# Prompt-stage barriers, loads and state moves, and narrower query products, in a one-core decoder step

## The chip, the cores and the metric

One core of one Trainium2 chip runs the whole program in one launch. The metric is device microseconds of one execution, median of the runs shown. The core's engines are TensorE (PE in the rows, PEld for its weight loads), VectorE (DVE), ScalarE (ACT), GpSimd (POOL) and SyncE (SP). Each runs its own list of instructions in order; they meet through semaphores. SP and GpSimd issue the DMAs, which all share 16 DMA engines.

## The reference

One layer of a decoder for a prompt of 512 positions and for 8 sequences with 4 new positions each (32 rows), model width 1024:

```
p   = x @ w_in                                   # q, k, v of 8 stick-breaking and 8 dilated-window heads
o   = concat(stick_breaking(...), merged dilated windows(...))
h1  = LayerNorm1(alpha * x + o @ w_out)
q   = (h1 @ peer_wq).reshape(tokens, 8, 2, 128)  # the query products
s   = einsum('nhcd,ckd->nhck', q, subkeys)       # 128 scores; top 16 of each, then top 16 of the 16 x 16 sums
y   = LayerNorm2(alpha * h1 + sum over the chosen experts e of gelu(h1 . u[e]) * gate * v[e])
```

Besides y it returns the new keys and values, and for each of the 8 sequences the window state (2048 rows of keys and as many of values), of which all but four rows are the old state shifted by four: that shift is a copy from memory to memory.

## The kernel before

All is float32. Where a product is split into a high and a low part (type FP32R), three products stand for one: high x high, high x low, low x high. The 544 tokens (512 and 32) lie in five tiles of 128, of which the last has 32 rows and 96 of padding.

The program is a list of stages. In each, every engine has a part, and `end_stage` closes it: the engine drains, adds 1 to the semaphore `over`, and waits until all five engines have done so. The stages that matter here, with the stretch of the profiled execution:

- **Projections** (0 to 209.8 us). SP loads x in one DMA, then the sample rows, the 128 x 640 constants `square` (identity, triangle, ones), the angles, and 24 blocks of `w_in`. TensorE transposes x into four PSUM banks, ScalarE copies the high part, VectorE subtracts the low part, and a bank is free for TensorE again when VectorE is done with it. VectorE begins with clearing buffers. GpSimd stores keys and values as they come out, the dilated keys and values with nine DMAs each.
- **Stick-breaking heads of the prompt** (209.8 to 310.9). SP loads the bias and `counts` (1 MB). For each of 8 heads TensorE makes the scores, VectorE the logits (L666), ScalarE the logarithms and exponents, TensorE the suffix sums, and at last TensorE weighs the values (L604) and ScalarE copies the result (L644).
- **Dilated heads of the prompt** (310.9 to 377.0): scores (L710), logits on VectorE (L770), exponents, transposes, weighing; then the results are transposed into `o_t` (ScalarE L815). Their buffers lie where those of the stage before lay.
- **Samples** (377.0 to 872.8): the 8 sequences against their pages and windows.
- **Norm** (872.8 to 965.1): SP loads the two rows of LayerNorm1, the subkeys and the first two blocks of `peer_wq`. TensorE multiplies each of five tiles by `w_out` (L1419), VectorE adds and normalises, TensorE transposes the result (L1410), which is split into parts: three tiles into `h1_r` and the other two, 256 columns, into `h1_rest`. TensorE is up to two tiles ahead of VectorE.
- **Query** (from 965.1): 8 blocks of `peer_wq` of 1 MB, two buffers. For each of 16 chunks of 128 query columns TensorE makes 24 products of 384 token columns and 24 of the rest (L1563), then the scores of the chunk before (L1548, plain f32). ScalarE copies; VectorE finds the top 16 of each score row. Block g + 2 is loaded when the low part of block g has been made. ScalarE's order has the high part of block 2 ahead of its copy of the first scores, and VectorE's has the first top-16 ahead of the low part of block 2. No barrier stands behind this stage: gates and experts follow as data allow.

The shift of the window state is 16 copies of 4 MB (`move_state`, L565), which GpSimd issues in four portions, `MOVES`, in the stages of the stick-breaking heads (once the counts are in), of the dilated heads, of the norm and of the query. After each portion GpSimd comes to its `end_stage`, but for the last.

Of the kernel before, what the change touches and what calls it, by code (L numbers as in the profile page):

```python
# [38 lines left out]
DB, DT = 8, 4  # L39
NS = DB * DT  # L40
N = SEQ + NS
NT = 5
NP = NT * P
H, HD = 8, 64
# [12 lines left out]
ND = 3 * P  # L57
# [108 lines left out]
def build(nc, x_prompt, x_sample, cache_k_sb, cache_v_sb, page_table, state_k_win, state_v_win,  # L166
# [4 lines left out]
    with ExitStack() as ctx:  # L171
# [75 lines left out]


        over = sem("stage_over")
        stage = {}  # L250

        def end_stage(eng):

            name = eng.engine
            stage[name] = stage.get(name, 0) + 1
            eng.drain().then_inc(over, 1)
            eng.wait_ge(over, 5 * stage[name])

        def clear_semaphores(sp):

# [37 lines left out]
        xs_rows = x_sample.rearrange("b t d -> (b t) d")  # L298
        w_in_g = w_in.rearrange("(e k p) (g c) -> g e p k c", e=2, p=P, c=WC)
        NG_IN = 2 * len(GROUPS)  # L300

        def rows_of(t):
            return P if t < NT - 1 else NS
# [6 lines left out]

        @part("sp")
        def _(sp):
            sp.dma_start(x_nat[:, 0:4, :], x_rows).then_inc(sem("x_prompt_in"), 16)
            sp.wait_ge(sem("tail_cleared"), 1)
            sp.dma_start(x_nat[0:NS, 4, :], xs_rows).then_inc(sem("small_in"), 16)
            sp.dma_start(sq, square).then_inc(sem("square_in"), 16)
            sp.dma_start(cos_sb, cosine).then_inc(sem("angles_in"), 16)
            sp.dma_start(sin_sb, sine).then_inc(sem("angles_in"), 16)
            sp.dma_start(pages_sb[:, :], page_table.rearrange("b j -> (b j)").rearrange("(o n) -> o n", o=1))\
              .then_inc(sem("pages_in"), 16)  # L320
            for g in range(NG_IN):
                for e in range(2):
                    if g >= 1:
                        sp.wait_ge(sem("w_low"), 2 * (g - 1) + e + 1)
                    sp.dma_start(w_sb[e], w_in_g[2 * COLUMN[GROUPS[g // 2]] + g % 2, e]).then_inc(sem(f"w_in_{e}"), 16)
# [27 lines left out]
        @part("pe")  # L353
        def _(pe):
            pe.wait_ge(sem("square_in"), 16)
            for t in range(NT):
                pe.wait_ge(sem("x_prompt_in" if t < 4 else "small_in"), 16)
                r = rows_of(t)
                for half in range(2):
                    u = 2 * t + half  # L360
                    if u >= 4:
                        pe.wait_ge(sem("x_low"), u - 3)
                    for k in range(4):
                        last = pe.transpose(bank(u % 4)[:, k * P:k * P + r],
                                            x_nat[0:r, t, (4 * half + k) * P:(4 * half + k + 1) * P],
                                            ident[0:r, 0:r])
                    last.then_inc(sem("x_t_ready"), 1)
            pe.wait_ge(sem("x_low"), 10)

            def turn(c, tiles):  # L370

                if c < 2:
                    pe.wait_ge(sem("proj_copied"), 10 * c + 10)
                else:
                    pe.wait_ge(sem("roped"), c - 1)
                for t in tiles:
                    v = 5 * c + t
                    if v >= 4:
                        pe.wait_ge(sem("qk_copied_dve"), v - 3)
                        if (v - 4) // 5 % 2 == 0:  # L380
                            pe.wait_ge(sem("q_copied_act"), 5 * ((v - 4) // 10) + (v - 4) % 5 + 1)
                    r = rows_of(t)
                    for pair in range(NPAIR):
                        last = pe.transpose(bank(4 + v % 4)[:, pair * P:pair * P + r],
                                            staged[c % 2][0:r, t, pair * P:(pair + 1) * P], ident[0:r, 0:r])
                    last.then_inc(sem("qk_ready"), 1)

            for c in range(len(GROUPS)):
                for g in (2 * c, 2 * c + 1):
                    pe.wait_ge(sem("w_low"), 2 * g + 2)  # L390
                    for t in range(NT):
                        u = NT * g + t
                        if u >= 4:
                            pe.wait_ge(sem("proj_copied"), u - 3)
                        r = rows_of(t)
                        n = 0
                        for k in range(KD):
                            for x, y in PARTS:
                                n += 1
                                last = pe.matmul(bank(u % 4)[0:r, 0:WC], lhsT=x_r[:, x, k, t * P:t * P + r],  # L400
                                                 rhs=w_in_r[g % 2][:, y, k, :], start=(n == 1), stop=(n == 3 * KD))
                        last.then_inc(sem("proj_ready"), 1)

                        if t == 1 and g % 2 == 0 and 2 <= c <= 5:
                            turn(c - 2, (NT - 1,))
                if 1 <= c <= 4:
                    turn(c - 1, range(NT - 1))
# [148 lines left out]
        bias = small[:, 0:8]  # L556
        bias_ht = small[:, 8:40].rearrange("p (h t) -> p h t", h=H)

        MOVES = (7, 4, 3, 2)

        def move_state(pool, turn):
            for n in range(sum(MOVES[:turn]), sum(MOVES[:turn + 1])):
# [123 lines left out]
                if h + 1 < H:  # L686
                    softplus(h + 1)

        for engine in programs:
            programs[engine].append(end_stage)  # L690


        PT_AT = (0, 1, 3, 6)
        dl_p = [take(WIDE, WORK)] + [take(WIDE)]
        dl_t = [take(WIDE) for _ in range(2)]
# [8 lines left out]
        @part("pe")  # L704
        def _(pe):
            def scores(h):
                if h >= 1:
                    pe.wait_ge(sem("dl_logits"), 4 * h)
                for qb in range(KB):
                    last = pe.matmul(bank(qb)[:, 0:(qb + 1) * P], lhsT=q_z["dil"][:, h, qb * P:(qb + 1) * P],  # L710
                                     rhs=k_t["dil"][:, h // 2, 0:(qb + 1) * P], start=True, stop=True)
                last.then_inc(sem("dl_scores"), 1)

            def weigh(h):
                pe.wait_ge(sem("dl_turned"), h + 1)
                if h >= 1:
                    pe.wait_ge(sem("dl_out_scaled"), h)
                for qb in range(KB):
                    for kb in range(qb + 1):
                        a = (PT_AT[qb] + kb) * P  # L720
                        c = qb * HD
                        last = pe.matmul(bank(7)[:, c:c + HD], lhsT=dl_t[h % 2][:, a:a + P],
                                         rhs=v_n["dil"][:, kb, h * HD:(h + 1) * HD], start=(kb == 0), stop=(kb == qb))
                last.then_inc(sem("dl_out"), 1)

            scores(0)
            for h in range(H):
                if h + 1 < H:
                    scores(h + 1)
                pe.wait_ge(sem("dl_exp"), 4 * h + 4)  # L730
                if h >= 1:
                    pe.wait_ge(sem("dl_turned"), h)
                for j in range(10):
                    last = pe.transpose(bank(4, 3)[:, j * P:(j + 1) * P], dl_p[h % 2][:, j * P:(j + 1) * P], ident)
                last.then_inc(sem("dl_turn"), 1)
                if h >= 1:
                    weigh(h - 1)
            weigh(H - 1)
# [21 lines left out]
        def _(dve):  # L760
            dve.wait_ge(sem("counts_in"), 2 * 16)

            def logits(h):

                dve.wait_ge(sem("dl_scores"), h + 1)
                if h >= 2:
                    dve.wait_ge(sem("dl_turn"), h - 1)
                for qb in range(KB):
                    a, w = PT_AT[qb] * P, (qb + 1) * P
                    dve.tensor_tensor_reduce(out=dl_p[h % 2][:, a:a + w], in0=bank(qb)[:, 0:w], in1=counts[:, qb, 0:w],  # L770
                                             scale=SCALE, scalar=LOWEST, op0=ALU.add, op1=ALU.max,
                                             accum_out=dl_max[h % 2][:, qb:qb + 1]).then_inc(sem("dl_logits"), 1)
                dve.wait_ge(sem("dl_logits"), 4 * h + 4)
                dve.tensor_scalar(dl_neg[h % 2], dl_max[h % 2], -1.0, None, ALU.mult).then_inc(sem("dl_neg"), 1)
# [34 lines left out]

        @part("act")  # L810
        def _(act):
            for u in range(8):
                t, half = u // 2, u % 2
                act.wait_ge(sem("o_t_ready"), u + 1)
# [653 lines left out]

        COLS = (ND, H1_REST)
        NC = 2 * PH
        NWQ = NC // 2
        place[0] = KEPT
# [58 lines left out]
        def _(pe):  # L1533
# [18 lines left out]
            for c in range(NC):  # L1552
                pe.wait_ge(sem("w_low"), 2 * NG_IN + c // 2 + 1)
                w = wq_r[c // 2 % 2]
                for half in range(2):
# [4 lines left out]
                    for x, y in PARTS[::-1]:  # L1560
                        for k in range(KD):
                            n += 1
                            last = pe.matmul(bank(u % 4)[:, 0:COLS[half]], lhsT=w[:, x, k, c % 2 * P:(c % 2 + 1) * P],  # L1563
                                             rhs=(h1_r, h1_rest)[half][:, y, k, :],
                                             start=(n == 1), stop=(n == 3 * KD))
                    last.then_inc(sem("pq_ready"), 1)
                if c >= 1:
# [787 lines left out]
```

## Time and profile before

| | us |
|---|---|
| median of 3 runs | 2494.16 (2484.43 to 2496.2) |
| profiled execution, its own time | 2485.89 |
| its span, first to last instruction | 2484.1 |
| TensorE busy | 2298.1 |
| VectorE busy | 1548.5 |
| ScalarE busy | 940.5 |
| GpSimd busy | 390.8 |

The profile is that of one execution. Busy time is an engine's own; waiting for a semaphore is not busy. A timeline row gives the start, the duration, the engine, the line, the operation, what is written from what, the number of instructions merged, and in brackets the idle time before it with what ended it. The landing of a DMA is counted from its issue.

### The profile page before, as it was taken

What the parts mean: (1) busy time and instruction counts of PE and PEld (TensorE: products, weight loads), DVE (VectorE), ACT (ScalarE), POOL (GpSimd) and SP (SyncE); (2) the same over time, 40 slices, a digit from 0 to 9 for tenths busy, and PEclk for the clock granted to TensorE, in tenths of its full rate; (3) what the DMA queues carried; (4) which work ended last, traced back from release to release, by engine and by line L of the source; (5) the groups of instructions that cost most, each with busy time, mean ns of one, the idle gap of its engine ahead of it and who ended that gap; (6) DMA issues with size and microseconds to landing.
All of it is one profiled execution on the core that took longest, in us unless ns stands there. A gap on an engine that the chain in (4) does not pass through costs nothing.

```text
span 2484.1 us, 37894 instructions
## 1 busy us (share of the span) xinstructions
PE 2298.1 (93%) x12921; PEld 1896.2 (76%) x12921; DVE 1548.5 (62%) x3167; ACT 940.5 (38%) x1432; POOL 390.8 (16%) x370
## 2 busy tenths in 40 slices
PE   7997887999999788998999879999999999999996
PEld 7996674666666436985577779999999999999995
DVE  3342331344434423769898877777777777777777
ACT  3224643445444401223356623333333333333332
POOL 0001000000000000000000043333333333333330
PEclk9998888989989888999999989999999999999998
DMA  4226985766666574303355699999999999999982
GB/s 129 87 88 204 304 270 186 233 194 208 209 212 215 171 255 143 97 25 97 99 197 183 235 344 322 314 314 313 313 315 313 311 312 311 314 313 312 311 294 82
DMA packets 224063, 568.20 MB, mean 229 GB/s; under 512 B 18017, under 2 KB 96418, under 8 KB 221282
## 3 DMA queue, kind: packets, MB, share of 16 engines
q1 hardware_dynamic: 174946, 327.75, 39.9%
q0 software_dynamic: 49024, 239.23, 27.7%
q8 instruction: 56, 0.92, 0.2%
q14 instruction: 37, 0.30, 0.0%
HBM read 528.24 MB, written 105.12 MB: 255 GB/s over the span
## 4 chain that ended last, share of the span: by engine, by line
PE 71%; DVE 6%; DMA 4%; SPq 2%; ACT 2%; issue 2%; DVEq 0%; ACTq 0%
PE psum L2067 21%; PE psum L2055 16%; PE psum L1842 6%; PE psum L1563 3%; PE psum L2045 3%; PE psum L999 3%; PE psum L1865 3%; PE psum L1071 2%; PE psum L1053 2%; PE psum L989 2%; PE psum L1419 2%; PE psum L1021 2%; DMA sample<-in_cache_v_sb_dram 1%; DMA peer<-in_ln_b_dram 1%; DMA peer<-in_peer_wq_dram 1%
## 5 line engine op out<-in xcount | busy, mean ns | idle before, releaser
L2067 PE MATMUL psum<-expert_parts 128*128 128x512 f32 x2304 | 550.5, 395 | 0.0
L2067 PEld LDWEIGHTS psum<-expert_parts 128*128 128x128 f32 x2304 | 427.0, 189 | 86.3 <-issue 0.8
L2055 PE MATMUL psum<-h_parts,expert_parts 128*128 128x384 f32 x2304 | 444.2, 341 | 2.9 <-DVE expert_parts L2172 1.5
L2055 PEld LDWEIGHTS psum<-h_parts,expert_parts 128*128 128x128 f32 x2304 | 402.9, 189 | 10.9 <-issue 1.8
L2119 ACT ACTIVATE expert_parts<-peer 128x1024 fp32r<-128x1024 f32 x128 | 135.8, 1061 | 359.1 <-PE psum L2067 322.2
L2172 DVE TENSOR_TENSOR expert_parts<-psum,expert_parts 128x512 fp32r<-128x512 f32 x192 | 132.7, 691 | 151.4 <-ACT expert_parts L2113 151.4
L2215 DVE SCALAR_TENSOR_TENSOR kept<-experts,kept 128x1024 f32<-128x1024 f32 x160 | 205.0, 1281 | 5.3 <-DVE kept L2205 3.0
L2030 POOL DMA_INDIRECT experts<-in_peer_v_dram,kept x160 | 188.5, 1178 | 70.1 <-issue 47.5
L1842 PE MATMUL psum<-h_whole,gate_table 128*128 128x384 f32 x512 | 179.0, 493 | 13.8 <-ACT gate_table L1894 13.8
L1326 DVE TENSOR_TENSOR sample_parts<-sample,sample_parts 128x512 fp32r<-128x512 f32 x128 | 85.1, 690 | 157.5 <-ACT sample_parts L1179 157.0
L400 PE MATMUL psum<-projection_parts 128*128 128x256 f32 (+1 forms) x1440 | 173.5, 282 | 3.8 <-DVE projection_parts L506 3.8
L400 PEld LDWEIGHTS psum<-projection_parts 128*128 128x128 f32 (+1 forms) x1440 | 169.6, 174 | 5.9 <-issue 3.9
L2113 ACT ACTIVATE expert_parts<-psum 128x512 fp32r<-128x512 f32 x192 | 115.0, 599 | 149.5 <-PE psum L2045 142.9
L2177 DVE TENSOR_TENSOR expert_parts<-peer,expert_parts 128x1024 fp32r<-128x1024 f32 x128 | 155.9, 1218 | 0.0
L1842 PEld LDWEIGHTS psum<-h_whole,gate_table 128*128 128x128 f32 x512 | 93.0, 192 | 69.9 <-issue 19.7
L2025 POOL DMA_INDIRECT experts<-in_peer_u_dram,kept x96 | 95.2, 992 | 322.8 <-DVE experts L2199 188.9
L1155 ACT ACTIVATE sample<-psum 128x512 f32<-128x512 f32 x128 | 75.9, 593 | 161.5 <-PE psum L989 161.3
L2025 POOL DMA_INDIRECT peer<-in_peer_u_dram,kept x62 | 80.4, 1297 | 357.7 <-DVE peer L2199 352.1
L999 PEld LDWEIGHTS psum<-attention,sample 128*128 128x128 f32 x1024 | 133.1, 202 | 1.4 <-issue 0.8
L2045 PE MATMUL psum<-kept,peer 128*128 128x128 f32 x768 | 116.1, 274 | 16.6 <-DVE expert_parts L2172 16.1
L999 PE MATMUL psum<-attention,sample 128*128 (+1 forms) x1024 | 129.4, 253 | 0.0
L2199 DVE SCALAR_TENSOR_TENSOR experts<-experts,kept 128x1024 f32<-128x1024 f32 x96 | 116.8, 1219 | 0.0
(281 smaller groups left out, 3261.9 us busy)
## 6 DMA issues: line engine op xcount, KB each, us to landing
peer<-in_peer_v_dram SPq DMA_DIRECT2D x128, 512.0 KB, 5.2
peer<-in_peer_u_dram SPq DMA_DIRECT2D x96, 512.0 KB, 5.4
sample<-in_cache_k_sb_dram SPq DMA_DIRECT2D x128, 256.0 KB, 3.1
sample<-in_cache_v_sb_dram SPq DMA_DIRECT2D x128, 256.0 KB, 2.9
out_dram<-in_state_k_win_dram POOLq DMA_DIRECT2D x8, 4088.0 KB, 35.6
out_dram<-in_state_v_win_dram POOLq DMA_DIRECT2D x8, 4088.0 KB, 33.8
gates_dram<-gate_table SPq DMA_DIRECT2D x12, 2048.0 KB, 7.1
experts<-gates_dram SPq DMA_DIRECT2D x32, 768.0 KB, 6.9
```

The lines of the kernel that those rows point to most:

```text
L400: last = pe.matmul(bank(u % 4)[0:r, 0:WC], lhsT=x_r[:, x, k, t * P:t * P + r], rhs=w_in_r[g % 2][:, y, k, :], start=(n == 1), stop=(n == 3 ...
L999: last = pe.matmul(bank(2)[:, c:c + 8].rearrange("p (e t) -> p e t", e=2), lhsT=k_turned[j % 2][:, pair, :], rhs=q_s["sb"][:, 2 * pair:2 * ...
L1842: last = pe.matmul(bank(6)[:, 0:ND], lhsT=early_t[e % 2][:, k, :], rhs=h1_f[:, k, :], start=(k == 0), stop=(k == KD - 1))
L2025: pool.indirect_dma_start(out=u_rows[p], out_offset=None, in_=peer_u, in_offset=index(q, p))\
L2030: pool.indirect_dma_start(out=v_rows[p], out_offset=None, in_=peer_v, in_offset=index(q - 1, p))\
L2045: last = pe.transpose(bank(7)[:, k % 4 * P:(k % 4 + 1) * P], u_sb[s][:, k * P:(k + 1) * P], ident)
L2055: last = pe.matmul(bank(6)[:, 0:ND], lhsT=u_t[s][:, a, k, :], rhs=h1_r[:, b, k, 0:ND], start=(k == 0 and n == 0), stop=(k == KD - 1 and n ...
L2067: last = pe.matmul(bank(2 * t + half), lhsT=weight[s][:, a, t * P:(t + 1) * P], rhs=v_r[s][:, b, half * 512:(half + 1) * 512], start=(firs ...
L2119: act.activation(v_r[s][:, 0, :], v_sb[s], ACT.Copy).then_inc(sem("v_high"), 1)
L2172: dve.tensor_tensor(u_t[s][:, 1, ks, :], bank(7).rearrange("p (k j) -> p k j", k=4), u_t[s][:, 0, ks, :], ALU.subtract).then_inc(sem("u_lo ...
L2177: dve.tensor_tensor(v_r[s][:, 1, :], v_sb[s], v_r[s][:, 0, :], ALU.subtract).then_inc(sem("v_low"), 1)
L2215: dve.scalar_tensor_tensor(y, v_rows[p], dots_act[:, p:p + 1], y, ALU.mult, ALU.add).then_inc(sem("added"), 1)
```

## The change

- GpSimd takes no part in the first barrier (`WITHOUT_POOL`); ScalarE waits for the stores of the dilated keys before it writes `o_t`, which lies over their buffer.
- The second barrier, between stick-breaking and dilated heads, is gone. In its place the dilated stage waits for single semaphores: TensorE's first scores, its first transposes, and VectorE's first two heads of logits.
- `square` is loaded first, and the x of the prompt in four DMAs, one per tile, each with its semaphore.
- `MOVES` goes from 7, 4, 3, 2 to 11, 0, 0, 5.
- The second products of each query chunk take 160 token columns (32 + 128) in place of 256; the 96 columns of padding are left out, in the products and in ScalarE's copy. `h1_rest` keeps its size.

```diff
+        WITHOUT_POOL = (1,)
         stage = {}
         def end_stage(eng):
             name = eng.engine
             stage[name] = stage.get(name, 0) + 1
+            if eng is nc.gpsimd and stage[name] in WITHOUT_POOL:
+                return
             eng.drain().then_inc(over, 1)
-            eng.wait_ge(over, 5 * stage[name])
+            eng.wait_ge(over, 5 * stage[name] - len([n for n in WITHOUT_POOL if n <= stage[name]]))
...
+        X_IN = ("x_prompt_in", "x_in_1", "x_in_2", "x_in_3", "small_in")
...
-            sp.dma_start(x_nat[:, 0:4, :], x_rows).then_inc(sem("x_prompt_in"), 16)
+            sp.dma_start(sq, square).then_inc(sem("square_in"), 16)
+            for t in range(4):
+                sp.dma_start(x_nat[:, t, :], x_rows[:, t, :]).then_inc(sem(X_IN[t]), 16)
             sp.wait_ge(sem("tail_cleared"), 1)
             sp.dma_start(x_nat[0:NS, 4, :], xs_rows).then_inc(sem("small_in"), 16)
-            sp.dma_start(sq, square).then_inc(sem("square_in"), 16)
...
-                pe.wait_ge(sem("x_prompt_in" if t < 4 else "small_in"), 16)
+                pe.wait_ge(sem(X_IN[t]), 16)
...
-        MOVES = (7, 4, 3, 2)
+        MOVES = (11, 0, 0, 5)
...
-        for engine in programs:
-            programs[engine].append(end_stage)
...
             def scores(h):
                 if h >= 1:
                     pe.wait_ge(sem("dl_logits"), 4 * h)
+                else:
+                    pe.wait_ge(sem("sb_logits"), H)
+                    pe.wait_ge(sem("sb_exponents"), H)
...
                 if h >= 1:
                     pe.wait_ge(sem("dl_turned"), h)
+                else:
+                    pe.wait_ge(sem("sb_out_copied"), H)
                 for j in range(10):
...
                 if h >= 2:
                     dve.wait_ge(sem("dl_turn"), h - 1)
+                else:
+                    dve.wait_ge(sem("sb_out"), H - 1 + h)
                 for qb in range(KB):
...
         def _(act):
+            act.wait_ge(sem("k_dil_out"), (1 + DB) * 16)
             for u in range(8):
...
-        COLS = (ND, H1_REST)
+        COLS = (ND, N - ND)
...
-                                             rhs=(h1_r, h1_rest)[half][:, y, k, :],
+                                             rhs=(h1_r, h1_rest)[half][:, y, k, 0:COLS[half]],
```

## Rows read from the trace of the kernel before

**Rows 1.** The page, busy time, share of the span and instructions of the engines.
```profile
PE 2298.1 (93%) x12921; PEld 1896.2 (76%) x12921; DVE 1548.5 (62%) x3167; ACT 940.5 (38%) x1432; POOL 390.8 (16%) x370
```
**Rows 2.** Table of stretches: stretch, length, busy us, granted clock, DMA share, GB/s.
```profile
872.80:965.10 92.30, 78.85 (x200) 37.24 (x200) 33.03 (x46) 11.11 (x22) 1.48 (x3) 0.89 0.52 172
965.10:1112.00 146.90, 139.83 (x933) 133.81 (x934) 86.54 (x465) 37.13 (x57) 0.99 (x2) 0.96 0.33 108
```
**Rows 3.** Timeline, start of the projections, VectorE.
```profile
13.00 5.20 DVE L512 TENSOR_TENSOR projection_parts<-psum,projection_parts 128x512 fp32r<-128x512 f32 x10
...
18.38 2.36 DVE L506 TENSOR_TENSOR projection_parts<-prompt,projection_parts 128x1024 fp32r<-128x1024 f32 x2 [0.18 <-ACT projection_parts L427]
```
**Rows 4.** GpSimd's drains, stretches 190:215 and 215:315 (ns min/median/max, first and last start).
```profile
L256 POOLq DRAIN  x1: 4057/4057/4057, 205.8 to 205.8; - x1
...
L256 POOLq DRAIN  x2: 52547/72128/91708, 219.1 to 312.7; - x2
```
**Rows 5.** Timeline around the first three barriers.
```profile
201.58 0.37 ACT L453 ACTIVATE attention<-psum 32x256 f32<-32x256 f32 x1 [2.36 <-PE psum L400]
...
209.87 0.35 SPq L573 DMA_DIRECT2D kept<-in_sb_logit_bias_dram  x1
...
215.92 1.55 DVE L666 TENSOR_SCALAR prompt_attention<-psum,kept 128x1280 f32<-128x1280 f32 x1 [34.11 <-DMA prompt_attention<-in_count_prompt_dram]
216.42 0.54 POOL L565 DMA_DIRECT2D out_dram<-in_state_k_win_dram  x1 [9.41 <-DMA prompt_attention<-in_count_prompt_dram]
...
303.24 0.38 ACT L644 ACTIVATE prompt_attention<-psum 128x256 f32<-128x256 f32 x1 [3.58 <-PE psum L604]
310.90 3.92 PE L710 MATMUL psum<-prompt 128*128 128x128 f32 x8 [7.70 <-SPq L256]
...
315.00 0.29 DVE L770 CUSTOM_DVE_ANT_0 prompt_attention<-psum,prompt_attention 128x128 f32<-128x128 f32 x1 [16.92 <-PE psum L710]
...
372.25 2.56 ACT L815 ACTIVATE kept<-psum 128x512 f32<-128x512 f32 x5 [0.17 <-PE psum L806]
```
**Rows 6.** DMA view, issues at 216.4, 873.2 and 969.4 us: KB, us to landing.
```profile
out_dram<-in_state_k_win_dram POOLq DMA_DIRECT2D x1, 4088.0 KB, 15.8
...
peer<-in_ln_b_dram SPq DMA_DIRECT2D x1, 512.0 KB, 30.3
...
peer<-in_peer_wq_dram SPq DMA_DIRECT2D x1, 1024.0 KB, 27.7
```
**Rows 7.** Timeline, norm stage, TensorE.
```profile
872.85 29.43 PE L1419 MATMUL psum<-w_out_sb,kept 128*128 128x512 f32 x64 [1.89 <-DVEq L256]
...
909.55 1.97 PE L1410 MATMUL psum<-kept 128*128 128x128 f32 x8 [7.28 <-DVE kept L1384]
...
911.32 15.59 PE L1419 MATMUL psum<-w_out_sb,kept 128*128 128x512 f32 x32
...
926.74 1.04 PE L1410 MATMUL psum<-kept 128*128 128x128 f32 x8
...
927.62 13.90 PE L1419 MATMUL psum<-w_out_sb,kept 128*128 128x512 f32 x32
```
**Rows 8.** DMA view, stretch 974:990: queue, packets, MB, share of 16 engines.
```profile
q0 software_dynamic: 96, 5.23, 99.6%
q1 hardware_dynamic: 96, 0.10, 3.1%
```
**Rows 9.** Timeline, query stage (and one weighing, 296.39).
```profile
296.39 2.34 PE L604 MATMUL psum<-attention,prompt_attention 128*128 128x64 f32 x20
...
969.43 81.86 SPq L1530 DMA_DIRECT2D peer<-in_peer_wq_dram  x6
...
994.05 1.16 PE L1548 MATMUL psum<-peer,kept 128*128 128x128 f32 x8
...
999.21 3.03 PE L1563 MATMUL psum<-h_rest,wq_parts 128*128 128x256 f32 x24
...
1006.76 6.00 PE L1563 MATMUL psum<-h_parts,wq_parts 128*128 128x384 f32 x24 [3.10 <-DVE wq_parts L1611]
```

## The prediction

> **What bounds the kernel now.** I read the page first. TensorE is busy 93% of the span and no other engine comes near it [rows 1], so on the whole TensorE sets the time; but the edits sit in the first 1.1 ms, where the table of stretches shows gaps [rows 2]: in the norm stage (872.8 to 965.1 us) TensorE is busy for 78.9 of 92.3 us, in the query stage (to 1112.0) for 139.8 of 146.9. Then I followed the order of time through each stage that the diff touches, and last the landings of the DMAs. Each stretch ends in another wait, so each edit has its own price.
>
> **Start: square first, x in four pieces.** TensorE's first transposes wait for the square now, so an earlier start looks worth some us. But VectorE clears buffers up to 13.0 us, then subtracts the x parts without a gap to 18.2, and the first weight part follows with 0.18 us of idle [rows 3]. TensorE's fifth group of transposes waits for VectorE's first subtraction (four banks), so whatever comes sooner in front of VectorE only waits there. I take 0; the cover is VectorE's clearing, and at most 0.2 us can come out. SP issues three more DMAs ahead of the first weight load, some 1.4 us, and that load is wanted at 17.3 us; 0 again.
>
> **First barrier without GpSimd.** GpSimd's drain before it runs from 205.8 to 209.9, since it holds until its stores of the last values have landed [rows 4]. ScalarE's last copy, which follows TensorE's last product, ends at 202.0. SP issues its next load at 209.87, the counts follow 0.4 later, and VectorE's first logits start at 215.92, when the counts land [rows 5]. Without GpSimd the barrier opens at about 202.5 (that copy and a short drain), the counts are issued at 202.9 and, at the same 5.6 us, land at 208.5. They now share the DMA engines with 1 MB of the values' stores: the bounds are 208.5 (no collision) and 210.7 (what is left of those stores goes first, 2.2 us). I take 209.6: **6.3 us gained**, between 5.2 and 7.4. ScalarE's new wait on the stores of the dilated keys, before the last transposes' copies, is for stores issued in mid-projections; 0.
>
> **Second barrier removed.** ScalarE's last copy of the stick-breaking heads starts at 303.24 and takes 0.4, yet TensorE starts the dilated scores only at 310.90 [rows 5]. The reason is again GpSimd's drain: it starts at 219.1 and takes 91.7 us, to 310.8, the landing of the seventh move of window state [rows 4]. After the change TensorE goes from the last weighing, which ends as that copy begins, straight to the scores, behind waits on values that this weighing has needed itself. They take 3.9 us as here, less if the clock stays up, so VectorE's first dilated logits start at 305.7 to 307.1 and not at 315.00. **8.5 us gained**, 7.9 to 9.3. The new waits of VectorE (previous head's weighing) and of TensorE's transposes (last copy, 303.6) end before that.
>
> **The moves of window state: 7, 4, 3, 2 become 11, 0, 0, 5.** GpSimd issues a move in 0.5 us; the first lands 15.8 us after its issue at 216.42, at 232.2, the seventh at 310.8, so one move takes (310.8 - 232.2) / 6 = 13.1 us [rows 4 to 6]. Eleven, issued from 210.1, end at 210.1 + 15.8 + 10 x 13.1 = 356.9. GpSimd's drain holds the next barrier until then; the other engines reach it when the copies that end at 374.81 are done [rows 5], now 14.8 us sooner, at 360.0. Cost 0, with 3 us of cover; should the moves be slower, each us beyond that is lost.
>
> In the norm stage three moves stand on the DMA engines when SP loads the norm's rows. The second of these rows lands after 30.3 us [rows 6], VectorE waits for it, and TensorE, two tiles ahead, stands for 7.28 us and then runs one turn at 1.97 us and one tile at 15.59, where the later ones take 1.04 and 13.90 [rows 7]. With no move there the row, half the size of the counts, lands in their 5.6 us or less, tile 0 is normalised some 6 us after its products are done (888 + 6 = 894), and TensorE, busy with tile 1 until 902.3, does not wait: 7.3 + 0.9 + 1.7 = **9.9 us gained** (7.3 if the two slow pieces stay).
>
> In the query stage five moves stand where two stood. Here the third weight block is issued at 969.43 and lands after 27.7 us, at 997.1 [rows 6, 9]. Why it is held can be counted: from 974 to 990 us the moves' queue passed 96 packets with 5.23 MB, the completion words among them, and SP's queue 96 with 0.10 MB [rows 8]. The queues alternate packet by packet, the moves' packets are some 64 KB and the load's 1 KB, and the load has 1024 of them. ScalarE waits for this block ahead of the first scores' copy, so VectorE's first top-16 and its low part of that block come later too, and TensorE's fifth chunk starts at 1006.76, 9.6 us after the landing, with 3.10 us of idle [rows 9]. Three moves more put all of this back by 3 x 13.1 = **39.3 us lost**. TensorE has its four chunks done at 1002 now and nothing else in its order. Nothing takes it back later: from here VectorE's top-16 follows TensorE chunk by chunk, and the gates follow VectorE. A page of the Trainium skill would have it otherwise: "DMA: Bandwidth & Descriptors", section "Queues, rings and completion order", says that an engine drains a packet of some 9 to 17 descriptors of one queue before it switches; by that the block's 64 pieces per engine would need 4 to 7 turns and land before five moves are through, with a sum of 2518. The row of 96 against 96 speaks for one piece a turn.
>
> **160 columns.** 16 chunks x 24 products go from 256 to 160 columns. At 256 the 24 take 3.03 us with the tail, 2.96 to the next instruction. What 160 cost no row shows: every FP32R product of this trace has 256 columns or more. From below: products of 64 columns, each a load of 128 weights and a product, run 20 in 2.34 us, 117 ns each [rows 9], so the loads hold the pace: 24 x 117 = 2.81 us, 0.15 less per chunk. If the loads didn't, 160/256 of 2.96 is 1.85, 1.1 less. From above: a plain f32 product of 512 columns costs two instructions, 32 in 13.90 us [rows 7], that is 869 ns or 1.70 ns per column; at this rate 160 columns are 272 ns, 24 of them 6.5 us, **3.55 us more per chunk**. The nearest rows in width, 128 columns, are all plain f32 and priced like that (8 instructions, four products, 1.16 us with the tail) [rows 9]; the pace of one column per cycle I see at 256 and up alone. I take the upper price and keep both ends. The first four chunks pay it inside the wait for the third weights (4 x 3.55 = 14 of 44 us idle); the other twelve pay 12 x 3.55 = **42.6 us lost**. ScalarE's shorter copies are behind TensorE; 0.
>
> A page speaks against this choice: the Trainium skill's "FP8 and Floating Point Precision", section "TensorE Precision Notes", gives four passes to true FP32 only and has reduced FP32 read as it is and truncated, without a word on width; by it the sum would be 2499. No row here has such a product.
>
> **Sum**, against the profiled execution, 2485.9 us with a span of 2484.1: -6.3 - 8.5 - 9.9 + 39.3 + 42.6 = +57.2, so 2543. The median of the three runs is 2494.2 (2484.4 to 2496.2), 8 above that execution; I name the sum's own figure.
>
> **The rivals.**
> - **The narrow products are not dear.** They run at the pace of the weight loads: -24.7 + 39.3 - 12 x 0.15 = +12.8, 2499; with nothing holding them -24.7 + 39.3 - 13.2 = +1.4, 2487. For it: at 256 columns a product takes 123 ns, hardly more than the 117 of one with 64 columns, so width itself may cost little. Against it: no FP32R width below 256 is shown. This one mechanism ends on the other side, within 0.5% of before; the point is a product of 117 ns, where 123 is the price now.
> - **The five moves do not hold the third weights.** The block then lands in time, and all 16 chunks pay the columns: -24.7 + 16 x 3.55 = +32, 2518. Against it: two stages show loads held, 30.3 us under three moves, 27.7 under two. It decides if the landing stays under some 30 us after the issue.
> - **Both of these:** -24.7 - 16 x 0.15 = -27, 2459, the one way to a faster kernel.
> - **The eleven moves hold the barrier** (slower by their lateness beyond 3 us): a few us on top of the forecast, inside its range.
>
> **Chances and range.** The forecast 0.58, with its own range 2530 to 2556 (ends of the gains together 4 us either way, a column price some 15% off, the median's 8 us). Cheap columns 0.27, weights not held 0.07, both 0.05, the rest 0.03. About 0.5%, 12.5 us, is what a measurement of this kernel can tell from no change. Cheap columns fall around that bound: I split them, 0.15 within and 0.12 slower. So faster 0.05, same 0.16, slower 0.79. From 2488 to 2556 lie the forecast, cheap columns and unheld weights, less some tails.
>
> **What would show each step.** VectorE's first logits near 209.6; dilated logits about 3 us after the copy at 303.24 starts there (11.8 now); GpSimd's drain to about 357; no wait on the norm's row; the third weights landing about 71 us after the query stage's start (32 now) and the fifth chunk at about 81; 24 narrow products in 6.5 us (or 2.8). The forecast is wrong if that last figure is near 2.8, or if the fifth chunk starts near 42 us into the stage.

## The result, and the profile after

| | kernel before | changed kernel |
|---|---|---|
| median | 2494.07 us (8 runs, 2484.43 to 2496.53) | 2509.38 us (8 runs, 2504.91 to 2512.23) |
| profiled execution | 2485.9 us, span 2484.1 | 2506.44 us, span 2504.6 |
| ratio | | 1.0069, 95% interval 1.0052 to 1.0086 |

Slower, as forecast, and inside the whole range (2488 to 2556), but below the forecast's own (2530 to 2556): by 15 us and not by 57. The median lies nearest to the rival "the narrow products are not dear" (+12.8 us). The changed lines stand some 5 to 9 lines further down than before (the query products are L1572, were L1563).

First the table of the two stretches that [rows 2] show for before: the norm stage and the query stage (their columns are those of [rows 2]).

```profile
866.10:948.20 82.10, 75.86 (x200) 35.93 (x200) 33.12 (x46) 11.24 (x23) 0.00 (x0) 0.96 0.12 40
948.20:1130.90 182.70, 138.22 (x929) 132.75 (x930) 85.71 (x459) 35.22 (x55) 2.46 (x5) 0.85 0.47 156
```

The norm stage lost its gap. In the query stage TensorE is busy for about as long as before, yet the stage has grown by some 36 us: the new time is idle time, not dearer products.

The start, and the first three stages, in the timeline (against [rows 3] and [rows 5]):

```profile
5.28 1.94 PE L369 MATMUL psum<-kept 128*128 128x128 f32 x8 [5.28 <-DMA kept<-in_x_prompt_dram]
...
13.00 3.21 DVE L517 TENSOR_TENSOR projection_parts<-psum,projection_parts 128x512 fp32r<-128x512 f32 x5
...
13.77 4.64 PE L369 MATMUL psum<-kept 128*128 128x128 f32 x24 [4.51 <-DVE projection_parts L517]
...
22.20 2.05 PE L405 MATMUL psum<-projection_parts 128*128 128x256 f32 x8 [3.80 <-DVE projection_parts L511]
...
203.28 0.37 ACT L458 ACTIVATE attention<-psum 32x256 f32<-32x256 f32 x1 [2.36 <-PE psum L405]
...
210.94 1.55 DVE L671 TENSOR_SCALAR prompt_attention<-psum,kept 128x1280 f32<-128x1280 f32 x1 [27.43 <-DMA prompt_attention<-in_count_prompt_dram]
...
298.02 4.58 PE L714 MATMUL psum<-prompt 128*128 128x128 f32 x8
298.26 0.38 ACT L649 ACTIVATE prompt_attention<-psum 128x256 f32<-128x256 f32 x1 [3.40 <-PE psum L609]
...
302.74 0.29 DVE L778 CUSTOM_DVE_ANT_0 prompt_attention<-psum,prompt_attention 128x128 f32<-128x128 f32 x1 [9.46 <-PE psum L714]
...
360.71 2.56 ACT L824 ACTIVATE kept<-psum 128x512 f32<-128x512 f32 x5 [0.26 <-PE psum L814]
...
365.54 0.18 DVE L1195 COPY kept<-kept 128x32 f32<-128x32 f32 x1 [8.59 <-SPq L266]
```

TensorE's rows of before, at the start:

```profile
10.14 6.95 PE L364 MATMUL psum<-kept 128*128 128x128 f32 x40 [10.14 <-DMA kept<-in_square_dram]
20.89 3.34 PE L400 MATMUL psum<-projection_parts 128*128 128x256 f32 x15 [3.80 <-DVE projection_parts L506]
```

TensorE turns x 5 us sooner, but VectorE still takes its first part at 13.00. TensorE stands 4.51 us for it, and its first projection product starts 1.3 us later than before. From ScalarE's last copy to the first logits are now 7.66 us (14.34 before), from the last stick-breaking copy to the first dilated logits 4.48 (11.76 before): both barriers are open sooner.

GpSimd's drain behind the eleven moves (ns min/median/max, first and last start):

```profile
L259 POOLq DRAIN  x1: 144676/144676/144676, 215.9 to 215.9; - x1
```

It ends at 215.9 + 144.7 = 360.6, before ScalarE's last copy at 363.27: the moves hold nothing here. TensorE's timeline of the norm stage, against [rows 7]:

```profile
866.17 29.20 PE L1428 MATMUL psum<-w_out_sb,kept 128*128 128x512 f32 x64 [1.90 <-DVEq L259]
...
895.21 1.04 PE L1419 MATMUL psum<-kept 128*128 128x128 f32 x8
896.08 13.90 PE L1428 MATMUL psum<-w_out_sb,kept 128*128 128x512 f32 x32
```

The wait of 7.28 us is gone, and the two slow pieces have become 1.04 and 13.90. The timeline of the query stage, which ScalarE begins at 948.20, against [rows 9]:

```profile
982.61 2.80 PE L1572 MATMUL psum<-h_rest,wq_parts 128*128 128x160 f32 x24
...
1019.26 1.91 ACT L1586 ACTIVATE wq_parts<-peer 128x2048 fp32r<-128x2048 f32 x1 [49.97 <-DMA peer<-in_peer_wq_dram]
...
1028.84 6.33 PE L1572 MATMUL psum<-h_parts,wq_parts 128*128 128x384 f32 x24 [3.92 <-DVE wq_parts L1620]
```

Two things can be read here. The fourth chunk's products are done at 985, and the fifth starts at 1028.84, 80.6 us into the stage (41.7 before), behind ScalarE's 50 us of waiting for the third weight block. And 24 products of 160 columns take 2.80 us, not the 6.5 of the forecast. The DMA view: the third block's landing, and the two queues between 972.5 and 992.5 (packets, MB, share of the engines), against [rows 6] and [rows 8]:

```profile
peer<-in_peer_wq_dram SPq DMA_DIRECT2D x1, 1024.0 KB, 66.7
...
q0 software_dynamic: 128, 6.28, 94.3%
q1 hardware_dynamic: 128, 0.13, 2.7%
```

The 2.80 us are the sign that the prediction named for being wrong. So the theory to test: the five moves cost the query stage some 39 us, the removed waits give back some 24, and the columns cost nothing. Its rivals: something other than the moves holds the third block; the columns are dear after all and hide in the stall.

### The profile page after: what moved, and what is told of

It is laid out like the page before. It is cut to its first block, busy times and chain, and to the rows that moved or that the text cites. A ratio compares the mean times of both kernels' runs of the same rounds, so it can differ in the third digit from the quotient of the medians.

```text
span 2504.6 us, 37893 instructions
## 1 busy us (share of the span) xinstructions
PE 2300.9 (92%) x12921; PEld 1899.6 (76%) x12921; DVE 1548.9 (62%) x3167; ACT 939.0 (37%) x1432; POOL 390.3 (16%) x370
## 4 chain that ended last, share of the span: by engine, by line
PE 81%; DVE 7%; ACT 3%; SPq 3%; DMA 2%; issue 2%; another core or an unknown queue 2%; DVEq 0%; ACTq 0%
PE psum L2076 20%; PE psum L2064 16%; PE psum L405 7%; PE psum L1851 6%; PE psum L1572 4%; PE psum L2054 3%; PE psum L1008 3%; PE psum L1874 3%; PE psum L1428 3%; PE psum L1080 2%; PE psum L1062 2%; PE psum L998 2%; DMA sample<-in_cache_v_sb_dram 2%; PE psum L1030 1%
```

## The experiments

**The five moves, put elsewhere.**

```diff
-        MOVES = (11, 0, 0, 5)
+        MOVES = (11, 0, 5, 0)
...
+            pool.wait_ge(sem("norms_in"), 2 * 16)
             move_state(pool, 2)
```

> The changed kernel with the five moves issued in the norm stage behind the landing of the norm's two rows, and none in the query stage. Theory (the moves alone hold the third weight block, the columns cost nothing): the third block lands some 12 us or less after its issue (66.7 in the changed kernel), TensorE does not stand before its fifth chunk, the query stage goes from 179.7 us back to 136 to 140, and the time is some 43 us under the changed kernel's 2509: 2466, 0.989 of before. Rival 1 (the stall is only moved): the first two weight blocks, or GpSimd's drain, are not through when the norm stage would end, and the stage grows by 10 us or more: 2480. Rival 2 (the narrow products cost the plain rate after all, hidden in the stall): 16 x 3.55 = 57 us come back out of it, 2520.

Measured: 2464.27 us, 0.9891 of before (0.986 to 0.9922). The query stage, from ScalarE's first weight copy to the last product's start, takes 135.7 us, where the changed kernel takes 179.9 and before 143.2; the norm stage stays at 82.1. TensorE's timeline at the fifth chunk, the landing of the third block, and GpSimd's drain behind the moves:

```profile
984.90 2.80 PE L1573 MATMUL psum<-h_rest,wq_parts 128*128 128x160 f32 x24
987.63 0.41 PE L1555 MATMUL psum<-peer,kept 128*32 128x128 f32 x2
987.97 1.16 PE L1558 MATMUL psum<-peer,kept 128*128 128x128 f32 x8
988.88 4.41 PE L1573 MATMUL psum<-h_parts,wq_parts 128*128 128x384 f32 x24
...
peer<-in_peer_wq_dram SPq DMA_DIRECT2D x1, 1024.0 KB, 5.5
...
L259 POOLq DRAIN  x1: 68012/68012/68012, 876.5 to 876.5; - x1
```

The block lands in 5.5 us and TensorE goes from chunk to chunk. The drain ends at 944.5, 6 us before ScalarE begins the query stage (950.48), so the moves are hidden where they now stand. They hold another load instead, the second weight block, issued at 870.24:

```profile
peer<-in_peer_wq_dram SPq DMA_DIRECT2D x1, 1024.0 KB, 74.5
```

It lands at 944.75 and is wanted only in the query stage, so this costs nothing, with less than 6 us to spare. The rivals fall: nothing else held the third block, the stall is not moved into the norm stage, and no dear columns came to light when it went.

**Fewer moves in front of the block.**

```diff
-        MOVES = (11, 0, 0, 5)
+        MOVES = (11, 0, 2, 3)
```

> The changed kernel with two of the five moves in the norm stage (not held back) and three in the query stage. Theory (each move ahead of the third block costs 13.1 us): the block lands 66.7 - 2 x 13.1 = 40.5 us after its issue and the fifth chunk starts at 80.4 - 26.2 = 54 us of the stage; the norm stage loses up to 10 us to the held row again, so 2509 - 26 + 7 = 2490, 0.998 of before. Rival (the block waits for all moves of a batch, or something else than the moves holds it): fifth chunk still near 80 us, time 2505 or more.

Measured: 2489.73 us, 0.9995 (0.9977 to 1.0014). The DMA view's landings of the third block and of the norm's second row:

```profile
peer<-in_peer_wq_dram SPq DMA_DIRECT2D x1, 1024.0 KB, 40.6
...
peer<-in_ln_b_dram SPq DMA_DIRECT2D x1, 512.0 KB, 30.1
```

The fifth chunk starts 54.5 us into the stage. With 27.7 us under two moves [rows 6], 40.6 under three and 66.7 under five, each move more costs 13 us, as the forecast had it. The norm's row is the other way: two moves hold it for 30.1 us, three for 30.3 [rows 6], and the norm stage takes 91.4 us again. The row goes in packets of 4 KB (127 with 0.50 MB in a stretch of the first experiment where no move runs), 128 for its 512 KB. Two moves are as many: 4088 KB in packets of 64 KB are 64 a move. It is also as many as one piece in the next experiment, which lands after 29.3 us. So the row lands with the second move, however many follow, and two moves cost the norm stage as much as three.

**The third block in eight pieces.**

```diff
+                pieces = [slice(k, k + 1) for k in range(KD)] if g == 2 else [slice(0, KD)]
+                for ks in pieces:
+                    sp.dma_start(wq_sb[g % 2][:, ks], wq_g[g][:, ks]).then_inc(sem(f"w_in_{g % 2}"), 16)
```

ScalarE's wait on the block counts the eight pieces.

> The changed kernel with the third weight block loaded in eight pieces of 128 packets of 1 KB instead of one load of 1024, so that each piece's landing is seen. Theory (the two queues pass packet for packet, some 5.5 a us each while moves run: 208 of the load's packets in 38 us in the changed kernel): the first piece lands some 23 us after its issue, the second some 46, and the other six together just after the last move, near 67; nothing changes in the time, 2505 to 2509. Rival 1 (a load stands wholly behind the moves that were issued before it): the first piece too lands only near 60 us or later. Rival 2 (each turn passes some ten of the load's packets): all eight are in by 30 us, and the stall goes.

Measured: 2499.71 us, a single run beside a single one of before, 2492.25, and so below the 2505 to 2509 expected; the fifth chunk still starts 80.5 us into the stage. Landings of the first and second piece and the median of two later ones; then the queues of 966 to 986 us, while the moves run, and of 1006 to 1014, when they end:

```profile
peer<-in_peer_wq_dram SPq DMA_DIRECT2D x1, 128.0 KB, 29.3
...
peer<-in_peer_wq_dram SPq DMA_DIRECT2D x1, 128.0 KB, 51.6
...
peer<-in_peer_wq_dram SPq DMA_DIRECT2D x2, 128.0 KB, 61.0
...
q0 software_dynamic: 135, 6.74, 98.5%
q1 hardware_dynamic: 137, 0.12, 3.0%
...
q1 hardware_dynamic: 1733, 1.67, 63.2%
q0 software_dynamic: 21, 0.33, 11.0%
```

The second piece takes 22.3 us longer than the first; the other six land between 1008.9 and 1013.5, around the end of the last move at 1010.6. Neither rival fits. The first two pieces are some 6 us later than I expected; why is open. Equal counts of packets (135 and 137) would also come of ten for ten, but the trace's single packets show turns of one: in the changed kernel, from 955 to 1010 us, where a packet starts just as another ends, the two are of different queues in 585 of the 595 cases that can be told. The section "Queues, rings and completion order" of the Trainium skill's page "DMA: Bandwidth & Descriptors", with its 9 to 17 descriptors (a typical figure, it says) drained from one queue before a switch, is not borne out by these two queues.

**The columns, back to 256 and alone.**

```diff
-        COLS = (ND, N - ND)
+        COLS = (ND, H1_REST)
```

> The changed kernel with 256 columns again in the query products of the last tiles. Theory (the pace of the weight loads, 117 ns a product at 160 columns against 123 at 256): 24 products take 3.03 us, not 2.80; four of the 16 chunks lie inside the stall, so 12 x 0.23 = 2.8 us more than the changed kernel: 2512, 1.008 of before. Rival (the price of my forecast, 272 ns a product): 43 us less, 2467.

> The kernel before with the 160 columns alone. Theory (pace of the weight loads): 24 products in 2.80 us instead of 3.03, of which the first four chunks' part goes into the wait for the third block: 12 x 0.23 = 2.8 us less, 0.999 of before, not to be told from it by the time. Rival (my forecast's price): 24 products in 6.5 us, the time 43 to 57 us up, 1.017 to 1.023 of before.

Measured: 2506.86 us, 1.0063 (1.0045 to 1.0081) for 256 columns in the changed kernel, and 2489.77, 1.0001 (0.9983 to 1.0018) for 160 in the kernel before. The groups of 24 products in TensorE's timelines, first of the one and then of the other:

```profile
1050.29 3.03 PE L1572 MATMUL psum<-h_rest,wq_parts 128*128 128x256 f32 x24
```

```profile
1021.53 2.80 PE L1563 MATMUL psum<-h_rest,wq_parts 128*128 128x160 f32 x24
```

The query stage takes 183.1 us with the 256 columns against 179.9 in the changed kernel, and 140.4 with 160 alone against 143.2 before: 3 us either way, near the 12 x 0.23 of the theory. So small a difference does not show in the medians. The 43 us of the forecast's price would have shown in both.

**The same 160 columns as plain f32.**

```diff
-  lhsT=w[:, x, k, c % 2 * P:(c % 2 + 1) * P],
-  rhs=(h1_r, h1_rest)[half][:, y, k, 0:COLS[half]],
+  lhsT=w[:, x, k, c % 2 * P:(c % 2 + 1) * P].bitcast((F32R, F32)[half]),
+  rhs=(h1_r, h1_rest)[half][:, y, k, 0:COLS[half]].bitcast((F32R, F32)[half]),
```

> The changed kernel with the 160-column products of the last tiles read as plain f32, so the type alone differs (their result is more exact, nothing is left out). Theory (the price of my forecast was the price of the other type): two instructions a product at 1.70 ns a column, 272 ns, so 24 products take 6.5 us instead of 2.80 and the 12 chunks outside the stall cost 12 x 3.7 = 44 us: 2550, some 1.024 of before. Rival (at 160 columns plain f32 goes by the pace of weight loads too, two instructions of 117 ns): 24 in 5.6 us, 12 x 2.8 = 34 us: 2540.

Measured: 2551.61 us, 1.024 (1.0223 to 1.0257). TensorE's timeline, 24 products and what follows:

```profile
1047.64 6.68 PE L1572 MATMUL psum<-h_rest,wq_parts 128*128 128x160 f32 x48
1054.26 0.41 PE L1554 MATMUL psum<-peer,kept 128*32 128x128 f32 x2
```

Twice the instructions, and (1054.26 - 1047.64) / 24 = 276 ns a product; the forecast had 272. So the price was right for plain f32, and the forecast put it on the wrong type.

**Narrower still.**

```diff
-        COLS = (ND, N - ND)
+        COLS = (ND, 64)
```

> The changed kernel with 64 columns in the query products of the last tiles: the queries of the last 96 tokens are left out, the copies of them too. Theory (the load of 128 weights sets the pace from 160 columns down): 24 products still take 2.80 us, 117 ns each. Rival (the columns still count): down by the same 0.23 us per 96 columns, 2.57 us.

Measured: 2506.88 us, a single run. This kernel leaves out the queries of the last 96 tokens. The group in TensorE's timeline:

```profile
1038.69 2.76 PE L1572 MATMUL psum<-h_rest,wq_parts 128*128 128x64 f32 x24
1041.38 0.41 PE L1554 MATMUL psum<-peer,kept 128*32 128x128 f32 x2
```

To the next instruction 2.69 us at 64 columns, 2.73 at 160, 2.96 at 256: 112, 114 and 123 ns a product. From 160 columns down the width hardly counts, and the rival's 2.57 us is not met; this fits a load of 128 weights that sets the pace, which no run changes by itself. The floor lies a little under the 117 ns of [rows 9].

**The two barriers, each alone in the kernel before.** One has the changed `end_stage` with `WITHOUT_POOL = (1,)` and ScalarE's wait on `k_dil_out`; the other leaves out the second `end_stage` and has the four waits that replace it.

> The kernel before with the first barrier without GpSimd (and ScalarE's wait on the stores of the dilated keys). Theory: from the end of ScalarE's last copy of the projections to VectorE's first logits 14.0 us become 7.3, as in the changed kernel, and GpSimd's drain still opens the second barrier, at the landing of the seventh move, which is issued 5 to 7 us sooner: so the time goes 5 to 7 us down, 0.9975 of before. Rival (the seventh move's landing does not come sooner, and the second barrier takes the gain back): dilated logits at 315 as before, no change.

> The kernel before without the second barrier. Theory: from the last stick-breaking copy to VectorE's first dilated logits 11.8 us become 4.5, as in the changed kernel, and GpSimd's drain, now behind eleven moves from 216.4, ends at 216.4 + 15.8 + 131 = 363 while the others are done at 367: 7.3 us gained at both the dilated logits and the sample stage's start, 0.997 of before. Rival (the eleven moves hold the next barrier): the sample stage starts at 377 as before, and nothing is gained.

Measured: 2483.43 us, 0.9968 (0.9953 to 0.9982), and 2484.0 us, 0.998 (0.9958 to 1.0002). Timeline of the first, at the second barrier:

```profile
304.27 4.23 PE L713 MATMUL psum<-prompt 128*128 128x128 f32 x8 [7.36 <-SPq L259]
```

Timeline of the second there, and GpSimd's drain in it:

```profile
304.75 0.38 ACT L644 ACTIVATE prompt_attention<-psum 128x256 f32<-128x256 f32 x1 [3.23 <-PE psum L604]
...
309.23 0.29 DVE L773 CUSTOM_DVE_ANT_0 prompt_attention<-psum,prompt_attention 128x128 f32<-128x128 f32 x1 [9.29 <-PE psum L709]
...
L256 POOLq DRAIN  x1: 141098/141098/141098, 222.0 to 222.0; - x1
```

With the first edit alone TensorE still stands 7.36 us for the drain, but the drain opens 6.6 us sooner than before (304.27 against 310.90), so this barrier does not take the gain back. From its first logits to the sample stage's first copy the dilated stage takes 61.9 to 66.7 us over all profiles, 62.1 before and 65.7 in this one, so only 2.7 us are left of it at the sample stage's start in this execution; the median is 6 us down. With the second alone the copy-to-logits time is the 4.48 us of the changed kernel, and the drain ends at 363.1, as worked out beforehand, ahead of the other engines (370.2). The interval of its ratio reaches 1, so its gain is shown by the profile rather than by the time.

**What covers the start.**

```diff
-            (four clearings of q_z, ahead of the x subtractions)
             w_low(0)
+            (the same four clearings)
             w_low(1)
...
-            act.wait_ge(sem("staged_cleared"), 7)
+            act.wait_ge(sem("staged_cleared"), 3)      # and 7 in q_copy
```

> The changed kernel with VectorE's four long clearings of the query buffers moved behind its first weight part (ScalarE's wait on them moved to its first copy into those buffers). Theory (VectorE's clearing is what the earlier x waits for): the first subtraction starts at 7 to 8 us instead of 13.0, ScalarE's and VectorE's turn of 0.86 us a half then ends near 16, and TensorE's first projection product starts at 18 to 19 instead of 22.2: 3 to 4 us gained in the profile, hardly to be told by the time (1.005 of before). Rival (the weights' load, or ScalarE, holds the first product): still 21 us or later.

> The same clearings moved, but x in one load and the square behind it, as in the kernel before: the first transposes still start near 10.1 us. Theory (with the cover gone, the order of the loads is worth what TensorE starts sooner): the first projection product 2 to 4 us later than in the run with the new order. Rival (something behind the transposes holds both): the same start in both.

Measured: 2499.41 us, 1.0043 (1.0021 to 1.0065), and for the old loads a single run, 2496.89 beside a median of 2488.9 before. The intervals overlap with the changed kernel's, so the profiles decide. Timeline with the new order of loads, and then with the old one:

```profile
7.07 0.69 DVE L514 TENSOR_TENSOR projection_parts<-psum,projection_parts 128x512 fp32r<-128x512 f32 x1 [3.52 <-ACT projection_parts L421]
...
16.34 7.94 PE L405 MATMUL psum<-projection_parts 128*128 128x256 f32 x43 [4.48 <-DVE projection_parts L508]
```

```profile
20.82 3.49 PE L403 MATMUL psum<-projection_parts 128*128 128x256 f32 x16 [3.80 <-DVE projection_parts L506]
```

The first projection product starts at 16.34, 5.9 us sooner than in the changed kernel and sooner than the 18 to 19 expected. With the old loads and the same clearings it starts at 20.82, where before it was 20.89. Neither edit gives anything without the other.

**Both edits that helped.** The moves of the first experiment and the clearings of this one:

> The five moves in the norm stage behind the norm's rows, and the clearings moved: both edits at once. Theory (the two lie in stages that do not touch): 2464 - 3.5 = 2460, 0.9875 of before. Rival (the sooner start is lost again at the barrier that GpSimd's eleven moves hold, whose cover is 3 us): 2464, 0.989.

Measured: 2450.7 us, 0.9841 (0.9818 to 0.9865), the fastest of all. That is some 9 us better than expected. The start gives 5.2 us of it instead of 3.5 (first projection product at 16.97); the rest I cannot assign beyond the spread of its runs (2448.36 to 2456.79).

## Why the forecast was right in its sign and wrong in its size

| step of the prediction | forecast, us | profile, us | |
|---|---|---|---|
| start | 0 | +1.3 | covered by the clearings, but not free |
| first barrier without GpSimd | -6.3 | -6.7 | right |
| second barrier removed | -8.5 (-7.9 to -9.3) | -7.3 | right cause, a little less in this profile |
| eleven moves | 0, 3 of cover | 0, 2.7 of cover | right |
| norm stage | -9.9 | -10.3 | right |
| five moves in the query stage | +39.3 | +39.0 | right |
| 160 columns | +42.6 | -2.3 | **the step that failed** |

**The 160 columns.** The step that failed is the sentence "I take the upper price and keep both ends". It priced a product of 160 columns at 272 ns, the rate of the plain f32 products, because those were the nearest rows in width. The product takes 114 ns. The twelve chunks behind the stall go from 101.6 to 99.3 us and gain 2.3 us; the term is off by 45 us, more than the whole error of the sum. The plain f32 run shows that the number belonged to the other type. The evidence for the other end was already in the text: 123 ns at 256 columns in the right type, and 117 ns as the pace of loads and narrow products. Two rows that near to each other leave the width little to decide, and a row of the same type should have weighed more than one of the same width. The rows of 128 columns, which the forecast took for its price, were no evidence for it either: 8 instructions take 0.91 us to the next (987.97 to 988.88 in the first experiment), 114 ns each, the pace of a load again. The sentence of the Trainium skill that spoke against the choice ("FP8 and Floating Point Precision", "TensorE Precision Notes": four passes for true FP32 only) agrees in its direction with the two runs at 160 columns, 114 and 276 ns; the passes themselves are in no row, which shows two instructions a product.

**The five moves.** This step carried the sign. Its numbers (landing 71 us into the stage, fifth chunk at 81) came out as 71.1 (ScalarE's start on the block) and 80.6, and the experiments take it apart: no moves 5.5 us, two 27.7, three 40.6, five 66.7, with the packets of both queues one for one.

**The barriers and the norm stage.** From copy to logits the first barrier gained 6.7 us, within its bounds; the logits start at 210.94 and not near 209.6, since the projections end 1.7 us later. At the second, TensorE starts the scores 0.24 us ahead of the last copy where it stood 7.66 us behind it, 7.9 gained; the scores themselves then took 4.7 us from their start to VectorE's first logits instead of 4.1, at a granted clock of 0.53 (298.0 to 302.8; near the lower level, 1.2 GHz) against 0.63 (310.9 to 315.0). I had hoped that a shorter wait would keep the clock up. It had fallen before the scores began, during the last weighing (0.50 from 296 to 298), and the term ends below its lower bound. That is partly chance: over the eleven profiles without this barrier the logits follow the copy by 3.3 to 4.5 us, and this one, with 4.48, is at the upper end.

**The start.** The cover was as described, and VectorE's first part did not move. But the zero took the wait to be free: TensorE stands 4.51 us in the middle of its transposes, and the last 24 then take 4.64 us at a granted clock of 0.50 (1.2 GHz; 13.7 to 18.5), where before the last 24 take 3.1 at 1.00 (2.4 GHz; 14.0 to 17.1). The first projection product starts at 22.20 instead of 20.89. In the seven profiles with the new loads and the clearings in their place it starts at 21.66 to 22.20, in the four with the old loads at 20.89 to 21.65, so the edit by itself loses some 0.8 us on average. With the clearings out of the way it is worth 4.5 us there (16.34 against 20.82) and 3.4 at the projections' last copy (198.30 against 201.72).

**What the profiles leave over.** The seven steps add up to +13.7 us by the profile; the spans differ by 20.5. The rest is 0.4 us more at the end of the projections, 0.7 in the dilated stage, 4.9 in the sample stage and 0.8 behind the query stage. No edit touches the sample stage, and it takes 491.7 to 504.5 us over the fourteen profiles (495.8 before, 500.6 in the changed kernel), so I count it as spread and not as an effect. The medians differ by 15.3.

## What to carry to other kernels

A price must come from a row of the same type before one of the same size: 123 ns at 256 columns in the right type, and the pace of the weight loads, bounded this one better than any row of the right width. When small and large transfers share the DMA engines, count packets: a load of 1 KB packets behind moves of 64 KB packets waits for the moves, so issue such moves where no load is wanted before they end, here behind the norm's rows, in 80 us in which the DMA engines were busy for 12% of the time. An edit that gives nothing because of a cover is not worthless, nor always free: name the cover, move it, and measure the two together.

## What the runs showed of the hardware

- While moves run, the two DMA queues pass one packet each in turn, whatever their size: 128 and 128 in 20 us, 6.28 MB against 0.13. When the moves end, the loads that they held follow at once: 1733 packets of the third weight block's rest and the fourth block in the 8 us from 1006 to 1014.
- A matrix product in FP32R of 64, 160 and 256 columns takes 112, 114 and 123 ns with its own load of 128 weights, at a granted clock of 1.00 (2.4 GHz); one of 160 columns in plain f32 takes 276.
- GpSimd's drain waits for all the moves that it has issued, up to 144.7 us, and a barrier that counts GpSimd waits with it.
- In the changed kernel TensorE stands for 4.51 us in the middle of its first transposes and does the rest at a granted clock of 0.50 (1.2 GHz): its earlier start with a gap ends 1.3 us later than the later start without one.
